# Transposes taken between the projection's units, and split activations and weights reordered around them, in a two-block transformer kernel

## What is computed

```python
def second_block(x, positions, ...):
    h = x
    for i in range(DEPTH_2):                       # 4
        a = rms_norm_2(h, attn_norm_g[i])
        if mixer == 0:   y = diff_attention(...)   # layers 0 and 3
        elif mixer == 1: y = moba_attention(...)   # layer 1
        else:            y = swa_sink_attention(...)  # layer 2
        h = h + y
        h = h + sqrelu_mlp(rms_norm_2(h, mlp_norm_g[i]), mlp_w_up[i], mlp_w_down[i])
    return rms_norm_2(h, final_norm_g)
```

## Time and profile before

| | us |
|---|---|
| three runs | 3692.72, 3706.13, 3708.25 |
| median | 3706.13 |
| profiled execution, its own time | 3687.08 |
| its span | 3685.3 |
| second block, from about | 2200 |
| PE busy over the span | 2596.3 (70%) |
| DVE busy | 2093.0 (57%) |
| ACT busy | 861.1 (23%) |
| granted PE clock, mean | 0.801 |

### The profile page before, as it was taken

The page is one execution under the profiler, slowest core; times in us unless marked ns, Lnnn a source line. Parts: engine busy times, 40 slices in busy tenths (PEclk is TensorE's granted clock), DMA queues, the critical chain, the costliest instruction groups (busy, mean ns, idle before and its releaser), DMA issues.

```text
span 3685.3 us, 34740 instructions
## 1 busy us (share of the span) xinstructions
PE 2596.3 (70%) x12127; PEld 1766.8 (48%) x12127; DVE 2093.0 (57%) x4607; ACT 861.1 (23%) x1319; POOL 963.8 (26%) x1028
## 2 busy tenths in 40 slices
PE   4987454545347985545545337899889979989898
PEld 2455222222003544222222006588778967977697
DVE  5565766666744546756666635655455554555554
ACT  0111111110001201101111005344434434444343
POOL 0001666656660003666666640000000000000000
PEclk9999677766658997677777668699969977998699
DMA  8753999999997545999999975145414431543153
GB/s 291 281 186 119 381 381 360 371 351 355 360 372 278 211 179 222 378 380 361 385 351 346 371 302 180 46 160 187 155 39 167 174 112 48 192 173 138 46 183 125
DMA packets 311927, 893.03 MB, mean 242 GB/s; under 512 B 22424, under 2 KB 32752, under 8 KB 311664
## 3 DMA queue, kind: packets, MB, share of 16 engines
q0 software_dynamic: 147456, 536.94, 37.9%
q1 hardware_dynamic: 164336, 354.45, 26.8%
HBM read 890.25 MB, written 1.05 MB: 242 GB/s over the span
## 4 chain that ended last, share of the span: by engine, by line
PE 53%; issue 13%; DVE 11%; POOL 8%; another core or an unknown queue 8%; DMA 4%; ACT 2%; SPq 1%; DVEq 0%; POOLq 0%; ACTq 0%
PE lin L606 8%; PE lin L885 6%; PE lin L887 6%; PE lin L886 6%; PE psS L793 4%; POOL proj L1928 4%; PE psS L643 3%; PE lin L837 3%; POOL ring L1941 2%; DVE proj L1684 2%; PE lin L672 2%; PE psT L885 2%; PE psT L586 2%; PE psT L887 2%
## 5 line engine op out<-in xcount | busy, mean ns | idle before, releaser
L1355 DVE TENSOR_TENSOR weights_split<-ring,weights_split 128x1024 fp32r<-128x1024 f32 (+1 forms) x376 | 451.8, 1208 | 514.6 <-ACT weights_split L1166 514.1
L1684 DVE CUSTOM_DVE_ANT_0 proj<-proj,psT 128x1024 f32<-128x1024 f32 x512 | 608.2, 1218 | 235.1 <-DMA proj<-in_expert_u,eidx 153.8
L1928 POOL DMA_INDIRECT proj<-in_expert_u,eidx x512 | 481.4, 940 | 851.8 <-DVEq L1658 661.6
L1166 ACT ACTIVATE weights_split<-ring 128x1024 fp32r<-128x1024 f32 (+1 forms) x376 | 391.8, 1046 | 569.3 <-PE lin L887 355.3
L837 PE MATMUL lin<-ring,rowb 128*32 128x512 f32 x896 | 212.4, 837 | 257.5 <-issue 111.7
L606 PE MATMUL lin<-ring,xT 128*128 128x512 f32 x768 | 336.1, 598 | 6.1 <-DVE xT L1307 3.5
L837 PE MATMUL lin<-vbuf,rowb 128*32 128x512 f32 x1024 | 212.8, 830 | 178.5 <-issue 92.8
L793 PE MATMUL psS<-xT,ring 128*128 128x256 f32 x1024 | 262.4, 415 | 41.0 <-issue 32.2
L1941 POOL DMA_INDIRECT vbuf<-in_expert_v,pT x256 | 239.9, 937 | 178.1 <-issue 77.4
L793 PEld LDWEIGHTS psS<-xT,ring 128*128 128x128 f32 x1024 | 211.8, 210 | 114.4 <-issue 74.4
L1941 POOL DMA_INDIRECT ring<-in_expert_v,pT x224 | 212.3, 948 | 182.9 <-PE lin L837 61.8
(11 more groups left out here) (246 smaller groups left out, 4743.3 us busy)
## 6 DMA issues: line engine op xcount, KB each, us to landing
ring<-in_mlp_w_up SPq DMA_DIRECT2D x32, 2048.0 KB
ring<-in_mlp_w_down SPq DMA_DIRECT2D x32, 2048.0 KB
ring<-in_ada_w SPq DMA_DIRECT2D x20, 2048.0 KB, 12.6
ring<-in_w_in SPq DMA_DIRECT2D x16, 2048.0 KB, 10.8
ring<-in_w_query SPq DMA_DIRECT2D x16, 2048.0 KB
ring<-in_diff_w_in SPq DMA_DIRECT2D x12, 2048.0 KB
ring<-in_moba_w_in SPq DMA_DIRECT2D x6, 2048.0 KB
ring<-in_w_attn_o SPq DMA_DIRECT2D x4, 2048.0 KB
```

The source lines that it names most:

```text
L1166: act.activation(part(p, 0, kind, w), raw_piece(slot, p, kind, w), ACT.Copy).then_inc(hi_ready, 1)
L1355: dve.tensor_tensor(part(p, 1, kind, w), raw_piece(slot, p, kind, w), part(p, 0, kind, w).bitcast(F32), ALU.subtract).then_inc(lo_ready, 1)
L1684: dve.tensor_tensor_reduce(ubuf[:, n % GB, :], ubuf[:, n % GB, :], x_row, 1.0, 0.0, ALU.mult, ALU.add, hdot[:, cb, k:k + 1]).then_inc(h_re ...
L1928: pool.indirect_dma_start(out=ubuf[:, (16 * cb + k) % GB, :], out_offset=None, in_=table["u"], in_offset=bass.IndirectOffsetOnAxis(ap=eidx ...
```

## The change

In the second block only:

- `row_groups` takes the place of `transposed_rows`. Two of the four groups are issued inside the unit before the norm (in `last_down` after piece 1 of its second half, in the output projection's second unit after piece 1), the other two inside the unit after it (after piece 0 of the projection, in `first_up` after piece 1 of its first pass). `first_up` goes over the four pieces twice, for the first and the last four blocks of k. ACT and DVE follow: two weight pieces, two groups of activations, two weight pieces, two groups (`high_with_xT`, `low_with_xT`), the second residual half among them.
- The output projection starts after the first group of attention rows; groups 3 and 4 stand behind pieces 0 and 1.
- In DIFF and MOBA the queries are transposed after the fourth unit and the keys after the fifth (`head_columns`), into the two banks of `psT` and the two of `psS`. The sixth unit's first piece stands before the attention loop, its other three in steps 2 to 4. ACT copies its result in step 4 and splits the output weights in steps 5 to 8; DVE makes their low pieces in the last steps.
- At the feed-forward's end ACT does `act_high(7, 1)` after two pieces.
- The DIFF head gain becomes a scale per column in `xT_high` and `xT_low`; the rows' factor is applied by two broadcast multiplications.
- `up` uses `psS` first and `psT` second; the opening matmuls of `lin` stand behind `up(1)`; one more small parameter DMA; an early square root on ACT.

```diff
+            def head_columns(C, b0, ready):
+                pe.wait_ge(qk_ready, ready)
+                for b in range(b0, b0 + 8, 2):
+                    if b0:
+                        pe.wait_ge(tr_used, C.tr - 3)
+                    for n in range(4):
+                        blk, t = b + n // 2, n % 2
+                        mm = pe.transpose(tr_bank(b)[:, n * P:(n + 1) * P], proj[:, t, blk * P:(blk + 1) * P], ident)
+                    mm.then_inc(tr_done, 1)
+                    C.tr += 1
...
                 for i in range(m.nsub + 4):
+                    if v_piece is not None and 2 <= i < NPC + 1:
+                        v_piece(i - 1)
...
+                        if v_piece is not None and o * m.width in (0, UC):
+                            pe.wait_ge(lin_used, C.lin - (o == 0))
...
+            def row_groups(C, first, used=None):
+                if used is None:
+                    pe.wait_ge(x_ready, 1)
+                else:
+                    pe.wait_ge(lin_used, used)
+                for k in range(2 * first, 2 * first + 4, 2):
+                    tr_group(C, [x[:, t, (k + b) * P:(k + b + 1) * P] for b in range(2) for t in range(NT)])
...
-                transposed_rows(C)
-                pe.wait_ge(tr_used, C.tr)
+                if i == 0:
+                    row_groups(C, 0)
+                tr0, lin0 = C.tr - 2, C.lin
+                def second_half(p):
+                    if p == 0:
+                        row_groups(C, 2, lin0 if i else None)
+                linear2(cols, tr0, second_half)
...
+                    for n in range(1, 4):
+                        linear2(cols)
+                    head_columns(C, 0, QK_BASE[i] + 1)
                     linear2(cols)
-                pe.wait_ge(qk_ready, i + 1)
-                attention(C, m)
+                    head_columns(C, 8, QK_BASE[i] + 2)
+                    attention(C, m, lambda p: linear_piece(UC, p))
...
-                tr_all(C, tokb)
-                pe.wait_ge(tr_used, C.tr)
-                for n in range(2):
-                    linear2(UC)
+                head_group(0)
+                head_group(1)
+                linear2(UC, tr1, later_heads)
+                linear2(UC, None, first_half)
...
+                def first_up(q0):
+                    if ub:
+                        pe.wait_ge(rl_done, ub - 1)
+                    for kh in range(2):
+                        for p in range(NPC):
+                            if kh == 0:
+                                pe.wait_ge(lo_ready, q0 + p + 1)
+                            if p == 0:
+                                pe.wait_ge(tr_used, tr2 + 2 + 2 * kh)
+                            for k in range(4 * kh, 4 * kh + 4):
+                                w = [ws[:, p, q, k * P:(k + 1) * P] for q in range(2)]
+                                mm = three(psS[:, p // 2, (p % 2) * S:(p % 2 + 1) * S], w,
+                                           (xh[:, k, :], xl[:, k, :]), k == 0 and p % 2 == 0, k == KC - 1)
+                            if kh == 1:
+                                mm.then_inc(pc_used, 1)
+                            elif p == 1:
+                                row_groups(C, 2, lin1 + 1)
...
                                 mm.then_inc(pc_used, 1)
+                                if p == 1 and i + 1 < DEPTH2:
+                                    row_groups(C, 0, C.lin + 1)
...
+            def high_with_xT(C, gains, kind="flat", w=D):
+                q0 = NPC * C.unit
+                slot, landed = C.next_slot()
+                high_at(slot, landed, q0, kind, w, first=(q0 == 0), pieces=range(0, 2))
+                xT_high(C, gains, 0, 4)
+                high_at(slot, landed, q0, kind, w, first=(q0 == 0), pieces=range(2, NPC))
+                xT_high(C, gains, 4, KC)
...
+                    def beside(i):
+                        if i == 4:
+                            projected(5, v_done)
+                        if 5 <= i < 5 + NPC:
+                            high_at(o_slot, o_landed, v_done, "flat", D, pieces=range(i - 5, i - 4))
...
-                high()
+                q0 = NPC * C.unit
+                slot, landed = C.next_slot()
+                high_at(slot, landed, q0, "flat", D, pieces=range(0, 2))
                 act_high(7, 1)
+                high_at(slot, landed, q0, "flat", D, pieces=range(2, NPC))
...
+            def low_with_xT(C, gains, second_half, early, kind="flat", w=D):
+                q0 = NPC * C.unit
+                slot, _ = C.next_slot()
+                low_at(slot, q0, kind, w, range(0, 2))
+                xT_low(C, gains, 0, 4)
+                low_at(slot, q0, kind, w, range(2, early))
+                if second_half is not None:
+                    second_half()
+                low_at(slot, q0, kind, w, range(early, NPC))
+                xT_low(C, gains, 4, KC)
...
                     dve.wait_ge(lin_used, C.lin + 2)
                     rope2(0, 16)
-                    for n in range(2):
-                        low(C)
+                    dve.sem_inc(qk_ready, 1)
+                    low(C)
+                    head_columns(C, m, 0)
                     dve.wait_ge(lin_used, C.lin + 4)
                     rope2(16, 16)
+                    dve.sem_inc(qk_ready, 1)
+                    low(C)
+                    head_columns(C, m, 8)
...
-                low(C)
-                attention(C, m)
+                    def after(n):
+                        if n < 3:
+                            low_at(o_slot, q0, "flat", D, range(n, n + 1 + (n == 2)))
+                    attention(C, m, after)
...
                     for t in range(NT):
-                        for h in range(8):
-                            sl = tokb[:, t, h * P:(h + 1) * P]
-                            ins = dve.scalar_tensor_tensor(out=sl, in0=sl, scalar=st[:, 44 + 8 * t + h:45 + 8 * t + h],
-                                                           in1=wrow[:, slot, :], op0=ALU.mult, op1=ALU.mult)
+                        rows = tokb[:, t, :].rearrange("p (h d) -> p h d", d=P)
+                        rstd = st[:, 44 + 8 * t:52 + 8 * t].rearrange("p (h d) -> p h d", d=1).to_broadcast([P, 8, P])
+                        ins = dve.tensor_tensor(rows, rows, rstd, ALU.mult)
```

More of the change, by code:

```diff
@@ L978, in _ @@
                 q = NPC * C.unit
-                up(0, 0, q)
+                first_up(q)
                 up(1, 1, q + NPC)
+                pe.wait_ge(lin_used, C.lin)
+                for b in range(4):
+                    pe.matmul(lin[:, b, 0:2], ident, cst("zero")[:, 0:2], start=True, stop=False, skip_group_check=True)
                 with pe.Fori(0, 3) as r:
@@ L1204, in _, with projected @@
-                high()
-                C.tr += m.nblk // 2
-                attention(C, m)
+                def projected(n, done):
+                    act.wait_ge(pc_used, done)
+                    pair = 2 * (C.lin % 2)
+                    for t in range(NT):
+                        a = act.activation(proj[:, t, n * UC:(n + 1) * UC], lin[:, pair + t, :], ACT.Copy, scale=st[:, 4 + t:5 + t])
+                    a.then_inc(lin_used, 1)
+                    C.lin += 1
+                C.tr += m.nblk // 2
@@ L1376, in xT_low, with head_columns, attention @@
                     C.tr += 1
-            def attention(C, m):
-                dve.wait_ge(qk_ready, 1)
-                for b in range(0, m.nblk, 2):
+            def head_columns(C, m, b0):
+                for b in range(b0, b0 + 8, 2):
+                    tr_copy(C, lambda c: qkT[:, b + c, :], None if b0 else (lambda c: m.scale), bank=tr_bank(b))
+            def attention(C, m, after=None):
+                for b in range(0, m.nblk if after is None else 0, 2):
                     if b < 8:
@@ L1407, in attention @@
                         probs(C, m, i - 1)
+                    if after is not None and i >= m.nsub:
+                        after(i - m.nsub)
                 C.sc += m.nsub
@@ L1811, in _ @@
                     dve.sem_inc(lam_x, 1)
-                    link(dve.tensor_scalar(wrow[:, slot, :], wrow[:, slot, :], 1.0 - LAM_INIT[i], None, ALU.mult))
-                low(C, w=2 * SWA_IN // NSWA if m is SWA else D)
-                xT_low(C, pcol[:, 8 * i:8 * i + 8])
+                    gain = pcol[:, 64 + 8 * slot:72 + 8 * slot]
+                    link(dve.tensor_scalar(gain, gain, 1.0 - LAM_INIT[i], None, ALU.mult))
+                done = NPC * C.unit
+                low_with_xT(C, pcol[:, 8 * i:8 * i + 8],
+                            (lambda: residual_half(C, 1, (pc_used, done), st[:, 2:4])) if i else None, 2,
+                            w=2 * SWA_IN // NSWA if m is SWA else D)
                 row_stats(C)
```

218 lines of the change are left out of this document (125 added, 93 removed).

## The result

The changed kernel takes 3536.9 us (median; 3533.4 to 3541.6) against 3699.4 (3691.7 to 3708.3) for the kernel before on the same chip: ratio 0.9553, 95% interval [0.9534, 0.9571], 4.5% faster. The profiled execution took 3533.4 (span 3531.6). The second block, from its first transposes (right behind the first block's final norm) to the end of the span, went from 1464.9 to 1300.5 us in the two traces: 164.4 gained, where I had summed 135.6. The first block, which is not changed, was 10.7 us longer in this trace than in the one before.

A forecast was written before the change was run, and what follows sets the result against it. PE bounds projections and feed-forward; waits between stages are mostly queue order. Entries 34.6, split 20.8, norm 36.0, output entry and head norm 9.7, attention 35, less 0.5 set-up, give 135.6 off 3706.1: forecast 3570 us, range 3545 to 3605.

The forecast's parts named there:

- the attention term: Queries, keys and last values reordered around the attention loop: gain 12 us (DIFF), 14 (MOBA), 35 for three layers after clock losses.
- The window from the fourth unit to the scores: From the fourth projection unit's end to the first attention scores: 35.8 us now, scores at +18.4 after the change.
- The two DIFF layers: Attention in each DIFF layer: 12 us gained, less 1 for an earlier clock fall, plus 1.85 for the head row norm.
- Entries: Layer entries, feed-forward's end to next projection: transposes inside neighbouring units remove the gaps; 34.6 us gained together.
- split: Last activation's split at the feed-forward's end, after two weight pieces instead of four: 5.2 us a layer, 20.8 in four.
- norm: Second norm, between output projection and up(0): transposes moved inside the units, no stall; 9.0 us a layer, 36.0 in four.
- the output projection's entry: Output projection's first unit starts after one group of transposes instead of four: 1.5 us a layer, 6.0 in four.
- (2): Rival: values in the attention give nothing, with pieces at 1.2 GHz and ACT late in the loop; 3608 us, chance 0.11.
- (3): Rival: transposes between units cool PE, seven blocks a layer with 1.9 us of slow clock each, 53 us; 3624, chance 0.05.
- (4): Rival: PE, running some 245 us without a pause from up(0) to the next projection's end, loses rate; 3727 us, chance 0.03.
- (5): Rival: the new orders on the queues collide and nearly all gain is lost; chance 0.01.
- the signs against: PE waits over 1 us in up(0) or first unit, ACT idle-free past step nine, MOBA loop over 5 us longer, feed-forward clock below 1.

## Why the prediction missed, point by point

**The step that failed** is the size of the attention term, "Three pieces of values, 8.2 us at full rate, move into the loop's first steps ... so part is covered", from which I took 14 for MOBA with bounds of -1.2 and 17.4. The window from the fourth unit to the scores was right (17.4 expected, 18.0 measured in MOBA). For loop and tail I had 3.4 us lost; they gave 10.2. I took the loop's own pace as fixed and asked only how much slower the pieces might run in it. That the pieces could set the pace of the loop was in neither bound, so "if all are hidden, 17.4" was no upper bound. The profile before held the sign: PE was full in the loop and yet at 0.55. A stage whose engine is full at half its clock can gain nearly half its length, less what is put in; here a step went from 3.58 to 1.95 us. The three experiments on MOBA (pieces moved out: +19.6; zeros put into the kernel before: -13.6; one pause: +13.3) show this cause. It is also what carries the time out of the range: with the pieces ahead of the loop MOBA's term would be 28.2 - 19.6 = 8.6, less than I forecast, and the whole about 3556. What the 14 lacked is thus the pace alone. The sum of the lower bound is also off: three pieces at half rate are 2 x 8.2 = 16.4, not 15.6, and the bound -2.0; nothing hangs on it.

**The two DIFF layers** gained 14.3 and 14.6 us, forecast 12.9. **Entries, split, norm and output** together gave 107.4 for 97.4 forecast, all too small: the output projection's entry by more than half (9.7 for 6.0), the others by 5 to 9%. The runs that undid two of them (split: 23.9 for 20.8; norm: 9.5 a layer for 8.1) agree with these signs; that the clock behind a gap costs more than I priced from the window right behind it is my reading, and no run isolates it.

**The base.** I started from 3706.1; the median on this chip came out at 3699.4, 6.7 us lower. With the 28.8 us of the block that makes 35.5; the miss was 33.1, and the rest is the first block.

**The rivals.** (2), values in the attention give nothing: wrong, the stretch gave 57.1 us in three layers, the largest term. (Its time takes off 38 where the sum holds 35; that would be 3605, the range's upper end.) (3), transposes cool PE: wrong. (4), PE loses its rate without rest: wrong. (5), the orders collide: wrong, every term gained. One window speaks against (3) and (4), from the first DIFF layer's output projection to 3.6 us behind the end of MOBA's loop:

```profile
2361.50:2672.00 310.50, 305.79 (x1822) 267.66 (x1821) 185.76 (x328) 157.33 (x234) 0.00 (x0) 1.00 0.44 156
```

310.5 us with PE busy for 305.8 of them and the clock at 1.00 throughout, with the blocks of transposes of a norm, an entry, the queries and the keys among them. A block of eight takes 1.03 us there and 1.94 at the block's first transposes (2231.10), where the clock is 0.50. I cited the Trainium skill ("TensorE: Matmul & The Clock Gate", Part 4: PE-mode transpose) for rival (3); this trace does not show the cooling that it would give for blocks of 1 to 2 us between dense matmuls.

**What I said would show it.** Waits for xT_low and act_split nearly gone: 5.1 left and none, yes. Those for the attention rows nearly gone: no, 17.6. I had costed the low pieces at the loop's end (3.0 us in DIFF, 1.5 in MOBA) and still listed this wait as one that goes. No window at 0.5 between output projection and next attention: MOBA's layer has none; SWA's, which keeps the old order there, is at 0.50 from 2918 us, 9 us ahead of its loop. Feed-forward unchanged: 157.8 with the opening matmuls now inside it, at 1.00. Of the signs against, one came true: PE waits over 1 us in a first unit for xT_low (3.2, in the first layer's entry); it also waits 1.5 for a low piece in SWA's second unit. ACT in MOBA's loop came near another: its first idle time behind its four pieces is 0.17 us in step 10, but PE never waits for ACT in that loop. The MOBA loop differs by more than 5 us, in the other direction.

## What to carry to other kernels

Before pricing work that moves into a stage, read that stage's clock: where PE is full at half clock, the question is not what the added work costs there but whether it keeps the clock up, and the bounds of the term must include that gain. A cheap test is a few useless matmuls in the first steps of the loop; here nine of them were worth 13.6 us in the kernel before, and those for SWA and DIFF give the changed kernel another 26. A loop that falls later, as DIFF's does, needs them in its later steps, and small enough not to cost what they bring. An "undo" must restore the order on every queue: one residual on the wrong side of four pieces on DVE changed the answer by 5.7 us.

## What the runs showed of the hardware

**One loop, two stable paces.** With the same instructions and PE never idle, a step of MOBA's loop takes 3.58 us in one kernel and 1.95 in another, and each pace held to the loop's end where nothing interrupted it. A pause of 3.50 us brought the slow one in and a full PE did not end it in the 28 us that were left. Full busy time is thus no sign of full clock. In the DIFF loops of the changed kernel waits of 0.9 us and less were followed by the same fall (0.52 in the last 28 us, PE busy 25.81). Why the loop's own matmuls hold either level but do not raise it is not settled by these runs.

**The chip.** The kernel before takes 3563 to 3565 us on three chips, and 3699 and 3710 in the other two comparisons, while the changed kernel's second block takes 1300.5 us on the first chip and 1300.1 on a faster one. The difference is in the first block, in its two stretches of indirect loads: 760.9 and 770.1 us in one trace of the changed kernel, 687.1 and 688.5 in the other. Windows of the first stretch, slower chip first:

```profile
345.20:1106.10 760.90, 374.70 (x1616) 159.04 (x1616) 487.00 (x1205) 75.31 (x114) 481.58 (x511) 0.68 0.95 366
```

```profile
349.00:1036.10 687.10, 296.97 (x1582) 144.93 (x1582) 485.41 (x1193) 75.09 (x113) 482.10 (x511) 0.68 1.02 404
```

The same loads run at 366 GB/s on the one chip and 404 on the other, with POOL, which issues them, busy for the same 482 us. What slows them no run shows.
